# Scores of two attention heads made in turn into two PSUM banks

## The chip, the core and the metric

The kernel runs on one NeuronCore of a Trainium2 chip. TensorE multiplies: it is loaded with a stationary operand (LDWEIGHTS), streams the moving one past it (MATMUL) and writes the product into PSUM, which has 8 banks of 512 f32 values per partition. VectorE (DVE) and ScalarE (ACT) read the banks; GpSimd (POOL) and SyncE (SP) do side work and issue DMAs. The engines run independently and wait for each other on semaphores. The metric is the device time of one execution in microseconds (us), a median over runs.

## What is computed

The reference runs two layers of a first block and two of a second, on 256 tokens of width 1024, in f32. Most of the work is dense projections. The change touches the attention scores of two places:

```python
# dilated attention, group 0 (dilation 1, radius 64): 16 heads of width 64
s = einsum('bqhd,bkhd->bhqk', q, k) * dh ** -0.5 + bias ; p = softmax(s) ; o = p @ v
# second block, differential attention: 8 heads x 2 softmax maps, width 64, causal
q = q.reshape(B, S, DIFF_HEADS, 2, DIFF_HEAD_DIM)      # k likewise; v is (B, S, 8, 128)
o = causal_block_attention(q, k, v, DIFF_HEAD_DIM ** -0.5)
o = o[..., 0, :] - lam * o[..., 1, :]
```

In the kernel each of the 8 x 2 maps is a head of its own, so both places have 16 heads of width 64. The second block runs twice (layers 0 and 1), so there are 16 dilated and 32 differential heads in all.

## The kernel before

`Kernel.order` writes one list of steps, `plan`. `program` walks it, and five generators (`sp_program`, `pe_program`, `act_program`, `dve_program`, `pool_program`) each emit their engine's part of a step, so every engine executes its part of the steps in the list's order. The main thread of the list is a stream of weight tiles: `mm` (12 matmuls of 512 columns, lines 1555 to 1557: weights are split into a high and a low part, `w_hi` and `w_lo`, and the product is made of three terms), followed by `split` for the tile four places on: ACT rounds it to `w_hi` (line 1780) as soon as TensorE is done with the tile whose buffer it takes, and then DVE subtracts to get `w_lo` (line 2060). In the mixers' attention every second `w_lo` is made by POOL (line 2724).

Between tiles a side thread puts attention in. `attention` is a software pipeline, one turn of its loop per weight tile: `scores` of head i, `turn_probs` of head i-1, `values` of head i-2.

- `scores`: TensorE takes a PSUM bank and makes the scores of both blocks of 128 queries (line 1623). Columns 0 to 255 of the bank hold block 1's queries against 256 keys, columns 256 on hold block 0's against 256 keys (dilated) or 128 (causal). DVE adds the bias and takes the maximum (line 2205) and frees the bank; ACT takes the exponential (line 1867).
- `turn_probs`: TensorE waits for the exponential and transposes the probabilities (line 1634), DVE or ACT copies them out (lines 2224, 1887).
- `values`: TensorE multiplies with v (line 1649). The heads of one group share a bank: four in the dilated stage, two in the differential one. Then `keep` or `diff` (line 2670) takes them out.

The operands of a head are 64 partitions high. `qt` and `kt` hold two heads in one chunk of 128 partitions: an even head on partitions 0 to 63, an odd one on 64 to 127 (`at = DH_A * (h % 2)` in the dilated stage, `r = slice(m * DIFF_D, (m + 1) * DIFF_D)` in the differential one). An f32 product that is no transpose shows in the trace as two LDWEIGHTS and two MATMUL records: two passes.

PSUM banks come from one ring, first freed, first taken. `Ring.take` hands TensorE the bank that was freed first, with the event that frees it, and TensorE waits for that event before its next instruction:

```python
bank, given = yield from banks.take(*name)
if given:
    q.wait_ge(*given)
```

One user of the ring is near the change: `oct_scores` (line 1681), the scores of the other two dilated groups. It makes 64x64 products of even and odd heads in turn, into two banks, in four combinations of 64 rows and 64 columns.

Of the kernel before, what the change touches and what calls it, by code (L numbers as in the profile page):

```python
# [17 lines left out]
SEQ = 256  # L18
# [371 lines left out]
class Kernel:  # L390
# [392 lines left out]

    def attention(self, heads, per_bank, by_whom, done):
        n = len(heads)
        for place, h in enumerate(heads):
            h.per_bank, h.place = per_bank, place % per_bank
            h.group = (by_whom, heads[place - h.place].uid)
        for i in range(n + 2):
            if i < n:  # L790
                if heads[i].bias is None:
                    heads[i].raw = self.stat(2)
                self.step("scores", heads[i])
                if heads[i].bias_no is not None and heads[i].bias_no + 6 < H_A:
                    self.step("load_bias", heads[i].bias_no + 6)
            if 0 <= i - 1 < n:
                heads[i - 1].by = self.by_turns()
                self.step("turn_probs", heads[i - 1])
            if i >= 2:
                h = heads[i - 2]  # L800
                self.step("values", h)
                if h.place == per_bank - 1:
                    done(h, i - 2 - h.place)
            yield
# [26 lines left out]
    def dilated(self, i, j):  # L831
# [3 lines left out]
        q, k = self.put("da_q", 0, [P, HALVES, D]), self.put("da_k", 8, [P, HALVES, D])  # L835
# [58 lines left out]
        def dense():  # L894
            yield from need(("v", 0, BLOCK), ("qt", 0, BLOCK), ("kt", 0, BLOCK))
            (qt, kt), v, heads = pairs[0], vs[0], []
            for h in range(H_A):
# [4 lines left out]
                    q=lambda half, c=h // 2, at=at: qt[at:at + DH_A, c, (1 - half) * P:(2 - half) * P],  # L902
# [8 lines left out]

            yield from self.attention(heads, 4, "da", keep)
            got["dense"] = [("vals", heads[-1].uid)]
# [317 lines left out]
    def mix(self, layer, _):  # L1231
# [213 lines left out]
        def attend(kind, per_bank, done):  # L1445
            heads = list(heads_of(kind))
            yield from self.attention(heads, per_bank, kind + L, done)
            got[kind, "vals"] = "vals", heads[-1].uid
# [73 lines left out]
def pe_program(k):  # L1522
# [9 lines left out]
    for what, *of in k.plan:  # L1532
# [6 lines left out]
        if what == "mm":  # L1539
            i, = of  # L1540
# [23 lines left out]
        if what == "mm_chunk":  # L1564
            i, = of
# [50 lines left out]

        if what == "scores":
            h, = of
            bank = yield from bank_for("scores", h.uid)
# [138 lines left out]
def act_program(k):  # L1758
# [8 lines left out]
    for what, *of in k.plan:  # L1767
# [90 lines left out]
        if what == "scores":  # L1858
            h, = of
            bank = yield from banks.of("scores", h.uid)  # L1860
# [178 lines left out]
def dve_program(k):  # L2039
# [11 lines left out]
    for what, *of in k.plan:  # L2051
# [130 lines left out]
        if what == "scores":  # L2182
            h, = of
            bank = yield from banks.of("scores", h.uid)
# [695 lines left out]
```

## Time and profile before

| | us |
|---|---|
| three runs | 2540.09, 2541.14, 2547.57; median 2541.14 |
| the profiled execution | 2539.82, of which the program's span is 2538.5 |
| TensorE busy | 2421.2 (95% of the span) |
| DVE busy | 1480.2 (58%) |
| ACT busy | 1194.4 (47%) |
| DMA | 161 GB/s from HBM over the span |

The 16 dilated heads of group 0 run from 309 to 395 us, the differential heads from 1558 to 1645 us (layer 0) and from 2106 to 2193 us (layer 1). The page gives engine shares over the whole span; what a change inside these three stretches is worth has to be read from the rows of the stretch: the start of one TensorE group to the start of the next gives what a block of work takes, and a bracket such as `[0.68 <-PE banks L1557]` gives how long an engine sat idle before a row, and which work ended that.

### The profile page before, as it was taken

What the parts mean: (1) busy time and instruction counts of PE and PEld (TensorE: products, weight loads), DVE (VectorE), ACT (ScalarE), POOL (GpSimd) and SP (SyncE); (2) the same over time, 40 slices, a digit from 0 to 9 for tenths busy, and PEclk for the clock granted to TensorE, in tenths of its full rate; (3) what the DMA queues carried; (4) which work ended last, traced back from release to release, by engine and by line L of the source; (5) the groups of instructions that cost most, each with busy time, mean ns of one, the idle gap of its engine ahead of it and who ended that gap; (6) DMA issues with size and microseconds to landing.
All of it is one profiled execution on the core that took longest, in us unless ns stands there. A gap on an engine that the chain in (4) does not pass through costs nothing.

```text
span 2538.5 us, 29689 instructions
## 1 busy us (share of the span) xinstructions
PE 2421.2 (95%) x11746; PEld 1957.6 (77%) x11746; DVE 1480.2 (58%) x2158; ACT 1194.4 (47%) x1754; POOL 281.5 (11%) x248
## 2 busy tenths in 40 slices
PE   7998999989999999999999999999999999999999
PEld 5786777768877877777787787777787877887787
DVE  4555556675555547766554577655565576645653
ACT  4443454344434445444444465554554455554543
POOL 1100010000000000000001112333101122333000
PEclk9998999989999999999999999999999999999999
DMA  6765544446556666544566554344556554445554
GB/s 206 204 182 151 175 119 117 144 122 190 175 173 184 181 182 181 160 141 144 176 184 182 181 170 143 108 125 158 179 175 209 179 160 123 117 131 159 169 174 146
DMA packets 211339, 411.36 MB, mean 162 GB/s; under 512 B 13690, under 2 KB 26890, under 8 KB 211200
## 3 DMA queue, kind: packets, MB, share of 16 engines
q1 hardware_dynamic: 204192, 388.55, 51.1%
q0 software_dynamic: 6576, 19.80, 2.9%
q8 instruction: 93, 1.52, 0.2%
q10 hardware_dynamic: 432, 1.11, 0.1%
q14 instruction: 46, 0.38, 0.1%
HBM read 408.31 MB, written 1.10 MB: 161 GB/s over the span
## 4 chain that ended last, share of the span: by engine, by line
PE 81%; DVE 11%; ACT 4%; DMA 2%; issue 2%; POOL 1%; ACTq 0%; DVEq 0%
PE banks L1555 24%; PE banks L1557 23%; PE banks L1556 23%; DVE w_lo L2060 3%; PE banks L1599 2%; ACT w_hi L1780 2%; PE banks L1649 2%; PE banks L1623 1%; PE banks L1634 1%; PE banks L1614 1%; DMA small<-in_diff_lambda 1%; POOL stat L2705 1%; DVE mx_merged L2693 1%; PE banks L1579 1%; PE banks L1580 1%
## 5 line engine op out<-in xcount | busy, mean ns | idle before, releaser
L2060 DVE TENSOR_TENSOR w_lo<-w_raw,w_hi 128x1024 fp32r<-128x1024 f32 x688 | 837.9, 1222 | 862.0 <-ACT w_hi L1780 859.2
L1780 ACT ACTIVATE w_hi<-w_raw 128x1024 fp32r<-128x1024 f32 (+2 forms) x744 | 781.0, 1053 | 974.6 <-PE banks L1557 922.5
L1555 PE MATMUL banks<-w_hi,xt_hi 128*128 128x512 f32 (+3 forms) x2112 | 848.2, 402 | 20.7 <-DVE xt_lo L2088 10.3
L1556 PE MATMUL banks<-w_lo,xt_hi 128*128 128x512 f32 (+3 forms) x2112 | 823.3, 390 | 0.0
L1557 PE MATMUL banks<-w_hi,xt_lo 128*128 128x512 f32 (+3 forms) x2112 | 822.5, 389 | 0.0
L1555 PEld LDWEIGHTS banks<-w_hi,xt_hi 128*128 128x128 f32 x2112 | 403.6, 191 | 111.3 <-issue 18.3
L1557 PEld LDWEIGHTS banks<-w_hi,xt_lo 128*128 128x128 f32 x2112 | 402.3, 190 | 89.1
L1556 PEld LDWEIGHTS banks<-w_lo,xt_hi 128*128 128x128 f32 x2112 | 403.6, 191 | 83.1 <-issue 3.1
L2705 POOL TENSOR_TENSOR stat<-stat,minus_half 128x1 f32<-128x1 f32 (+2 forms) x60 | 54.6, 916 | 1052.4 <-DVE stat L2147 731.3
L2724 POOL TENSOR_TENSOR w_lo<-w_raw,w_hi 128x1024 fp32r<-128x1024 f32 x56 | 134.3, 2399 | 304.4 <-ACT w_hi L1780 304.3
L1555 PE MATMUL banks<-w_hi,ffn_ht_hi 128*128 128x512 f32 x352 | 141.9, 403 | 3.3 <-DVE w_lo L2060 3.3
L1557 PE MATMUL banks<-w_hi,ffn_ht_lo 128*128 128x512 f32 x352 | 140.5, 399 | 0.0
L1556 PE MATMUL banks<-w_lo,ffn_ht_hi 128*128 128x512 f32 x352 | 140.5, 399 | 0.0
L1555 PE MATMUL banks<-w_hi,mlp_ht_hi 128*128 128x512 f32 x256 | 102.2, 399 | 1.2 <-DVE w_lo L2060 1.2
L1557 PE MATMUL banks<-w_hi,mlp_ht_lo 128*128 128x512 f32 x256 | 101.5, 396 | 0.0
L1556 PE MATMUL banks<-w_lo,mlp_ht_hi 128*128 128x512 f32 x256 | 101.4, 396 | 0.0
L1555 PEld LDWEIGHTS banks<-w_hi,ffn_ht_hi 128*128 128x128 f32 x352 | 67.0, 190 | 19.5 <-DVE w_lo L2060 3.7
L1557 PEld LDWEIGHTS banks<-w_hi,ffn_ht_lo 128*128 128x128 f32 x352 | 67.0, 190 | 16.4
L1556 PEld LDWEIGHTS banks<-w_lo,ffn_ht_hi 128*128 128x128 f32 x352 | 67.1, 191 | 15.8
L1599 PE MATMUL banks<-ident,tok 128*128 128x128 f32 x212 | 35.2, 312 | 39.4 <-DVE tok L2068 39.4
L1867 ACT ACTIVATE probs<-probs,mx_nmax 128x256 f32<-128x256 f32 x96 | 42.9, 448 | 63.0 <-DVE mx_nmax L2205 62.8
L1599 PEld LDWEIGHTS banks<-ident,tok 128*128 128x128 f32 x212 | 28.0, 159 | 47.1 <-issue 30.0
(382 smaller groups left out, 2550.0 us busy)
## 6 DMA issues: line engine op xcount, KB each, us to landing
w_raw<-in_w_mlp SPq DMA_DIRECT2D x128, 512.0 KB, 3.8
w_raw<-in_w_in SPq DMA_DIRECT2D x104, 512.0 KB, 3.7
w_raw<-in_ffn_w_gate SPq DMA_DIRECT2D x88, 512.0 KB, 3.7
w_raw<-in_ffn_w_up SPq DMA_DIRECT2D x88, 512.0 KB, 3.8
w_raw<-in_ffn_w_down SPq DMA_DIRECT2D x88, 512.0 KB, 3.7
w_raw<-in_attn_w_in SPq DMA_DIRECT2D x72, 512.0 KB, 3.8
w_raw<-in_ret_w_in SPq DMA_DIRECT2D x64, 512.0 KB, 3.9
w_raw<-in_ret_w_out SPq DMA_DIRECT2D x16, 512.0 KB, 3.9
```

The costliest lines, as they stand in the source:

```text
L1555: pe.matmul(bank, xh, wh, start=(c == 0), stop=False)
L1556: pe.matmul(bank, xh, wl, start=False, stop=False)
L1557: mm = pe.matmul(bank, xl, wh, start=False, stop=(c == b.chunks - 1))
L1579: pe.matmul(bank, xh, hi[:, cols], start=(t.k0 == 0), stop=False)
L1580: pe.matmul(bank, xh, lo[:, cols], start=False, stop=False)
L1599: mm = pe.transpose(bank[:, j * P:(j + 1) * P], src(t.half, s), order)
L1649: mm = pe.matmul(out[:, at:at + h.dv], pt[:, kh, s, :], h.v(kh), start=(kh == 0), stop=(kh == n_keys - 1))
L1780: act.activation(k.w_hi[i % SPLIT][:, 0:m], k.raw[i % RAW][:, 0:m], ACT.Copy).then_inc(*ev.mark(k.w_hi_made, ("w_hi", i)))
L1867: act.activation(row, row, ACT.Exp, bias=h.nmax[:, s:s + 1], scale=-1.0, accum_out=h.den[:, s:s + 1]).then_inc(*done)
L2060: dve.tensor_tensor(lo, raw, hi.bitcast(F32), ALU.subtract).then_inc(*ev.mark(k.w_lo_made, ("w_lo", i)))
L2705: pool.tensor_tensor(out, mean, k.minus_half[:, 0:n], ALU.pow).then_inc(*ev.mark(k.pool_done, name))
L2724: pool.tensor_tensor(lo, raw, hi.bitcast(F32), ALU.subtract).then_inc(*ev.mark(k.w_lo_pool, ("w_lo", i)))
```

## The change

`attention` gets an argument `paired`, true in the two places. For an even head it emits a new step `scores_pair`, in which TensorE makes the scores of the even and of the odd head: it takes a bank for each, and issues block 1 of the even head, block 1 of the odd head, block 0 of the even head, block 0 of the odd head. The step `scores` of both heads stays in its place for DVE and ACT; TensorE passes over it. The products are the same and so are their operands. The other attentions (cross, latent) are not paired.

```diff
-    def attention(self, heads, per_bank, by_whom, done):
+    def attention(self, heads, per_bank, by_whom, done, paired=False):
...
-                self.step("scores", heads[i])
+                if paired and i % 2 == 0:
+                    self.step("scores_pair", heads[i], heads[i + 1])
+                self.step("scores", heads[i], paired)
...
-            yield from self.attention(heads, 4, "da", keep)
+            yield from self.attention(heads, 4, "da", keep, True)
...
-            yield from self.attention(heads, per_bank, kind + L, done)
+            yield from self.attention(heads, per_bank, kind + L, done, kind == "diff")
...
-        if what == "scores":
-            h, = of
+        if what == "scores_pair":
+            both = []
+            for h in of:
+                both.append((yield from bank_for("scores", h.uid)))
+                for e in h.after:
+                    q.wait_ge(*(yield from ev.of(*e)))
+            for s in range(2):
+                for h, bank in zip(of, both):
+                    mm = pe.matmul(bank[:, s * SEQ:s * SEQ + h.keys(s)], h.q(1 - s), h.k[:, 0:h.keys(s)], start=True, stop=True)
+                    if s == 1:
+                        mm.then_inc(*ev.mark(k.pe_done, ("scores", h.uid)))
+
+        if what == "scores" and not of[1]:
+            h, _ = of
```

On TensorE, at the dilated stage's first heads (`da_kt`, `da_qt` are the transposed keys and queries, `probs` the probabilities that are transposed; the weight tile's rows between them repeat), before:

```order
L1623 MATMUL banks<-da_kt_142,da_qt_141 128x256 x2
L1555 MATMUL banks<-w_hi_56,xt_hi 128x512
...
L1623 MATMUL banks<-da_kt_142,da_qt_141 128x256 x2
L1634 MATMUL banks<-ident,probs_72 128x128 x4
L1555 MATMUL banks<-w_hi_53,xt_hi 128x512
...
L1623 MATMUL banks<-da_kt_142,da_qt_141 128x256 x2
L1634 MATMUL banks<-ident,probs_73 128x128 x4
L1649 MATMUL banks<-da_v_145,probs_t_75 128x64 x4
```

and after (line 1627 is the new step, 1648 the transposes, 1663 the values):

```order
L1627 MATMUL banks<-da_kt_142,da_qt_141 128x256 x4
L1557 MATMUL banks<-w_hi_56,xt_hi 128x512
...
L1648 MATMUL banks<-ident,probs_72 128x128 x4
L1557 MATMUL banks<-w_hi_53,xt_hi 128x512
...
L1627 MATMUL banks<-da_kt_142,da_qt_141 128x256 x4
L1648 MATMUL banks<-ident,probs_73 128x128 x4
L1663 MATMUL banks<-da_v_145,probs_t_75 128x64 x4
```

The second head's two products now stand beside the first head's, and the second turn of the loop goes from the weight tile straight to the first head's transposes.

On TensorE in layer 0's differential heads 10 and 11, with what each instruction waits for (`mx_mq` are transposes for the latent attention), before:

```order
L1614 MATMUL banks<-ident,mx_mq_201 96x128 x3
L1623 MATMUL banks<-mx_kt_209,mx_qt_208 128x256 [waits dve_done]
L1623 MATMUL banks<-mx_kt_209,mx_qt_208 128x128
L1634 MATMUL banks<-ident,probs_74 128x128 [waits act_done,dve_done]
L1634 MATMUL banks<-ident,probs_74 128x128 x2
L1649 MATMUL banks<-mx_v_206,probs_t_75 128x128 [waits dve_done]
```

and after:

```order
L1616 MATMUL banks<-ident,mx_mq_201 96x128 x3
L1627 MATMUL banks<-mx_kt_209,mx_qt_208 128x256 [waits dve_done]
L1627 MATMUL banks<-mx_kt_209,mx_qt_208 128x256
L1627 MATMUL banks<-mx_kt_209,mx_qt_208 128x128 x2
L1648 MATMUL banks<-ident,probs_74 128x128 [waits act_done,dve_done]
L1648 MATMUL banks<-ident,probs_74 128x128 x2
L1663 MATMUL banks<-mx_v_206,probs_t_75 128x128 [waits act_done]
```

The pair has taken the ring's bank that the transposes would have had, so everything behind it gets a bank that is freed later: `turn_probs` of head 9 the one that `diff` of heads 6 and 7 frees (line 2670, on DVE), and `values` of head 8 the one that ACT frees when it copies out the first `mx_mq` transposes (line 1821). The rows of DVE, ACT, POOL and SP stand in the same order before and after.

## Rows read from the trace of the kernel before

**Rows 1.** Busy time by stretch: length, PE, PEld, DVE, ACT, POOL, PEclk, DMA, GB/s.

```profile
309.00:395.00 86.00, 85.47 (x452) 66.67 (x451) 46.97 (x100) 42.88 (x98) 10.37 (x20) 1.00 0.45 117
1558.00:1645.00 87.00, 82.06 (x443) 66.68 (x444) 54.89 (x148) 49.23 (x118) 27.61 (x14) 0.98 0.38 107
```

**Rows 2.** Line 1623: count, duration ns min/median/max, first and last start, shapes.

```profile
L1623 PE MATMUL banks<-da_kt,da_qt x64: 376/376/480, 309.8 to 391.0; 64*128 64x256 f32 x64
```

**Rows 3.** PE in order of time, dilated heads: start us, us, what.

```profile
313.53 0.40 PE L1557 MATMUL banks<-w_hi,xt_lo 128*128 128x512 f32 x1
313.85 1.13 PE L1623 MATMUL banks<-da_kt,da_qt 64*128 64x256 f32 x4
314.91 0.66 PE L1634 MATMUL banks<-ident,probs 128*128 128x128 f32 x4
```

**Rows 4.** PE in order of time, layer 0's differential heads.

```profile
1619.79 0.40 PE L1556 MATMUL banks<-w_lo,xt_hi 128*128 128x512 f32 x1
1620.03 0.40 PE L1557 MATMUL banks<-w_hi,xt_lo 128*128 128x512 f32 x1
1620.35 0.92 PE L1623 MATMUL banks<-mx_kt,mx_qt 64*128 64x256 f32 x4
1621.20 0.55 PE L1634 MATMUL banks<-ident,probs 128*128 128x128 f32 x3
```

**Rows 5.** Line 1681 at 404 us: whole group, then its records up to 404.435 and 404.460.

```profile
404.33 1.16 PE L1681 MATMUL banks<-da_kt,da_qt 64*64 64x64 f32 x64
...
L1681 PE MATMUL banks<-da_kt,da_qt x4: 267/267/268, 404.3 to 404.4; 64*64 64x64 f32 x4
...
L1681 PE MATMUL banks<-da_kt,da_qt x8: 218/242/268, 404.3 to 404.5; 64*64 64x64 f32 x8
```

**Rows 6.** Waits from 309 to 395 us: total us, times, longest; then the first of them.

```profile
ACT w_hi L1780 <- PE banks L1557: 7.0, 10, 1.3
...
309.40 1.06 ACT L1780 ACTIVATE w_hi<-w_raw 128x1024 fp32r<-128x1024 f32 x1 [1.17 <-PE banks L1557]
```

**Rows 7.** One turn of the dilated loop in order of time, ACT and PE.

```profile
340.52 1.05 ACT L1780 ACTIVATE w_hi<-w_raw 128x1024 fp32r<-128x1024 f32 x1
...
345.07 0.49 ACT L1867 ACTIVATE probs<-probs,da_nmax 128x256 f32<-128x256 f32 x1
...
346.34 1.06 ACT L1780 ACTIVATE w_hi<-w_raw 128x1024 fp32r<-128x1024 f32 x1 [0.68 <-PE banks L1557]
...
346.95 0.66 PE L1634 MATMUL banks<-ident,probs 128*128 128x128 f32 x4
```

**Rows 8.** Transposes of differential heads 4, 6 and 8 of layer 0 on PE.

```profile
1581.97 0.52 PE L1634 MATMUL banks<-ident,probs 128*128 128x128 f32 x3 [2.17 <-DVE mx_kcat L2625]
...
1592.15 0.55 PE L1634 MATMUL banks<-ident,probs 128*128 128x128 f32 x3
...
1603.50 0.52 PE L1634 MATMUL banks<-ident,probs 128*128 128x128 f32 x3 [1.70 <-ACT probs L1867]
```

**Rows 9.** ACT: the exponential of head 6 ends; the rounding before head 8.

```profile
1591.45 0.19 ACT L1867 ACTIVATION_READ_ACCUMULATOR probs<-probs,mx_nmax 128x1 f32 x1
...
1596.26 1.06 ACT L1780 ACTIVATE w_hi<-w_raw 128x1024 fp32r<-128x1024 f32 x1 [2.22 <-PE banks L1557]
```

**Rows 10.** What frees the banks at heads 10 and 11; PE's values of head 8.

```profile
1610.69 0.69 DVE L2670 TENSOR_TENSOR tmp<-banks,stat 128x512 f32<-128x512 f32 x1
1611.71 0.67 ACT L1821 ACTIVATE mx_mqt<-banks,gain_columns 96x512 f32<-96x512 f32 x1
1611.55 0.83 PE L1649 MATMUL banks<-mx_v,probs_t 128*128 128x128 f32 x6
```

**Rows 11.** Stretches behind PE's long waits, columns as in rows 1.

```profile
1582.00:1590.00 8.00, 7.48 (x41) 6.17 (x42) 4.98 (x16) 5.10 (x12) 2.45 (x2) 1.00 0.24 66
1604.00:1608.00 4.00, 4.00 (x16) 3.39 (x15) 1.63 (x2) 2.86 (x5) 2.10 (x1) 0.57 0.01 4
2130.00:2134.00 4.00, 3.62 (x15) 3.36 (x16) 1.92 (x6) 3.20 (x8) 1.88 (x1) 0.62 0.00 0
```

More of the change, by code:

```diff
@@ L1858, in act_program @@
         if what == "scores":
-            h, = of
+            h, _ = of
             bank = yield from banks.of("scores", h.uid)
@@ L2182, in dve_program @@
         if what == "scores":
-            h, = of
+            h, _ = of
             bank = yield from banks.of("scores", h.uid)
```

## The prediction

> **What bounds the kernel now.** I read the page first: TensorE is busy for 95% of the span, the next engine, DVE, for 58% (the table above). Then the busy times by stretch for the places with paired heads: PE 85.5 us of 86.0 at the dilated heads, 82.1 of 87.0 at layer 0's differential heads, where it idles for 5 us [rows 1]; layer 1's stretch reads alike. So a TensorE microsecond counts there as far as the other engines can follow. Third comes PE's order of time, for what a group of scores takes between its neighbours; fourth the brackets on ACT and PE, for who waits for whom.
>
> **What a group of scores takes.** Tile matmuls start 0.24 us apart (1619.79 and 1620.03 [rows 4]). At the dilated heads the last of a tile starts at 313.53, so PE is free at 313.77, and the transposes start at 314.91: 1.15 us for the scores between them [rows 3]. The group's four passes of 256 columns last 1.13 us and the last alone 0.376, so four starts span 0.757; the first pass is 0.104 longer than the others (480 against 376 ns [rows 2]), which leaves 0.217 us per pass. Four passes are 0.87 us, so 0.28 us go to entering and leaving the group. At a differential head PE is free at 1620.27 and the transposes start at 1621.20: 0.94 us [rows 4]. Two passes of 0.217 and two of half that are 0.65, and again 0.29 is left for entering and leaving.
>
> **What the pair takes.** The edit removes every second group and doubles the passes of the other, with rows 0 to 63 and rows 64 to 127 in turn. No row of before has products 128 columns wide on the two row halves in turn. The nearest is line 1681, which uses both row halves and both column halves: four of its records have started by 404.36, no more until 404.435, and the next four by 404.460; its 64 records last 1.16 us, one of them 0.218 [rows 5]. That is (1.16 - 0.218) / 64 = 15 ns per record, where a pass of 64 columns needs 217 / 4 = 54 ns: four at once, among them two that share their columns and differ in rows. The bounds for the pair: eight passes as long as four (full overlap), or as long as eight (none). I take full overlap, because what two full-width halves share, the columns' way out into two banks, line 1681 shares already. A pair then lasts as long as a single group now, and saves 1.15 us dilated and 0.94 us differential: 8 x 1.15 + 16 x 0.94 = 24.2 us of TensorE, if all of it is kept.
>
> The Trainium skill (TensorE: Matmul & The Clock Gate, Part 3, What overlaps and what doesn't) says that matmuls are strictly first in, first out in their starts and ends. By that, the second pass of one head would hold up the first pass of the next, which is a rival below. The trace speaks against it: each product has two passes, and still four records start together.
>
> **Dilated: what keeps up.** In each turn of the pipeline there is a second loop without TensorE: ACT rounds the next tile (340.52), DVE subtracts and then adds the bias, ACT takes the exponential (its second half at 345.07), and only behind that comes ACT's next rounding (346.34) [rows 7]. TensorE needs 5.4 us per turn (81.2 us between the first and the last of 16 score groups, 309.8 to 391.0 [rows 2]), and would need 4.8. What the loop has to spare is what ACT's roundings wait for TensorE: 7.0 us in the stretch, of which 1.17 lie before the first head [rows 6], so 5.8. The exponential is over at 345.56 and its transposes start at 346.95 [rows 7]: a margin of 1.4 us, from which the odd head's group between them, 1.15, is now taken. So PE will stand before some even heads' transposes, 0.1 to 0.3 us each, and be held to the loop's pace. At the end it may have used up part of the margin; I take 0.4. Of 9.2 us offered, 5.8 + 0.4 = **6.2 us** are kept.
>
> **Differential: what keeps up.** Between the heads DVE and ACT also do the latent attention's norms, and PE stands 2.17 us before the transposes of head 4 and 1.70 before those of head 8 [rows 8]. Layer 0 by pairs, heads 0 to 15:
> - 0 and 1: head 0's exponential is the last thing that its transposes wait for already; 0.
> - 2 and 3: 0.94 gained and lost again before head 4, whose exponential hangs on DVE and ACT waiting for each other; 0.
> - 4 and 5, 8 and 9: PE stands before the first head's transposes; 0.
> - 6 and 7: head 6's exponential is over at 1591.64, its transposes start at 1592.15 [rows 8, 9]; 0.45 gained. It lasts, since the rounding before head 8 waits 2.22 us for PE [rows 9] and moves up with it.
> - 10 to 15: no wait stands before the even heads' transposes, and the norms are done; 3 x 0.94 = 2.8.
> - The new waits: the values of head 8 need the bank that line 1821 frees at 1612.38, and PE reaches them at 1611.55. Before them head 9's transposes need the one that line 2670 frees at 1611.38 [rows 10], which is no later than they start now. Behind the waiting values stands the next tile, and ACT has moved up as far as PE: 0.8 us, of which I count 0.7.
>
> That is 0.45 + 2.8 - 0.7 = 2.6 us. Layer 1 has the same heads in the same order, and I take it alike: **5.2 us** together.
>
> **The clock.** Behind the wait that ended at 1603.50 the next 4 us ran at a granted clock of 0.57, behind layer 1's wait before head 4 at 0.62, and behind the wait that ended at 1581.97 at 1.00 [rows 11]. These waits grow, since the odd head's group no longer stands in them: 2.17 to about 3.7 us with the 0.7 that was gained before. I expect that one to be followed by a dip to 1.2 GHz too: 4 us x 0.43 = 1.7, of which 0.2 lie under the next wait, -1.5 us. In the dilated stretch waits stay too short for that.
>
> **What costs nothing.** DVE, ACT, POOL and SP keep their order. The odd head's scores lie one turn longer in their bank, which the ring of 8 bears everywhere but at heads 8 and 9. DMA moves 107 to 117 GB/s in these stretches [rows 1] and would have to move 8% more; were that cover gone, PE would wait for weight tiles, which it nowhere does there.
>
> **The sum.** 6.2 + 5.2 - 1.5 = 9.9 us off the profiled execution's 2539.8, which is 2529.9. The median of the runs is 1.3 above that execution, so I predict **2531 us**.
>
> **Rivals.**
> - *Half overlap*, 2533. Passes start strictly in order, so a head's second pass runs beside the next head's first: five slots for four, and a pair saves 0.93 dilated and 0.72 differential. Dilated 8 x 0.93 = 7.4 is still above what the loop gives, about 5.7; differential 2 x (0.45 + 3 x 0.72 - 0.7) = 3.8; clock -1.5: 8.0 off. Rows 5 speak against it.
> - *No overlap*, 2538. Full-width products take turns whatever their rows, so the edit doesn't do what it is about; a pair saves one entering and leaving, 0.28: 8 x 0.28 + 2 x (4 x 0.28 - 0.7) = 3.1 off. For it: no row shows two full-width products at once.
> - *Everything kept*, 2517. The other engines follow, 24.2 us off. Against it stand the waits of rows 6 and 8.
> - *Slower*, 2551. Each change of the row half costs what entering and leaving a group costs, 0.28, and nothing overlaps: a pair has three changes and saves one, so it is 2 x 0.28 = 0.56 us longer than two groups are now, 8 x 0.56 + 10 x 0.56 where PE decides, 10 us in all. It decides from a dilated pair longer than 2.3 us. Line 1681 changes halves at every product and shows none of it [rows 5]. The Trainium skill (TensorEngine Tiling (Array Packing), Key Properties) has a drain at a change of tiling mode, "not just tile"; by that too a pair would enter and leave once.
>
> **Chances.** Forecast 0.62, half overlap 0.12, no overlap 0.13, everything or most of it kept 0.09, slower 0.04. Within the forecast the loops may leave 5 to 8 us dilated and 2 to 8 differential, with none to three more dips: 2525 to 2537. A measurement of this kernel can tell a difference of about 0.3%, 7.6 us, from no change. Faster by more: 0.50 + 0.07 + 0.09 = 0.66; within: 0.30; slower by more: 0.04. The range holds the first three cases and some of the fourth: 2522 to 2539.
>
> **What would show it.** The pair's group on PE with its 8 records: 1.1 us long (dilated) and 0.9 (differential) is full overlap, 1.35 and 1.15 half, 2.0 and 1.6 none. In the dilated stretch ACT's roundings hardly wait for PE, PE stands briefly before even heads' transposes, and from the first score group to the last transposes some 6 us are gone, not 9. PE waits 3 us and more before differential head 4, 2.5 before head 8, and the values of head 8 wait. I am wrong in kind if a dilated pair is longer than 1.5 us, and in size if the dilated stretch gives 9 us or a differential one more than 5.

## The result, and the profile after

| | before | after |
|---|---|---|
| median of six runs each, in turn on one chip | 2541.86 (2539.31 to 2547.57) | 2528.67 (2525.50 to 2530.80) |
| the profiled execution / its span | 2539.82 / 2538.5 | 2530.56 / 2529.3 |
| predicted | | 2531 (2522 to 2539) |

The ratio is 0.9945, with a 95% interval of 0.9931 to 0.9958: faster, by more than 0.3%. The two profiled executions are 9.3 us apart, the medians 13.2. In the tables below one of diff_only's eight executions took 2989.8 us at a mean granted clock of 0.75, against about 0.98 in all the others; its median counts it, its ratio does not.

The page of the changed kernel, TensorE's line (busy us, share of the span): 22 us less work than the 2421.2 before, where the pairs offered 24.2.

```profile
PE 2399.1 (95%) x11746; PEld 1946.4 (77%) x11746; DVE 1486.8 (59%) x2158; ACT 1193.3 (47%) x1754; POOL 281.7 (11%) x248
```

So the work is gone nearly as counted, and in the profiled execution more than half of it, 12.9 us, came back as waiting. The two stretches of [rows 1] (columns as there) say where: TensorE now idles for 2.7 us at the dilated heads (0.5 before) and 8.4 at layer 0's differential heads (4.9 before).

```profile
309.00:395.00 86.00, 83.30 (x490) 66.99 (x488) 49.18 (x102) 44.67 (x102) 10.38 (x20) 1.00 0.47 127
1558.00:1645.00 87.00, 78.60 (x448) 65.12 (x447) 59.09 (x143) 47.77 (x112) 30.45 (x16) 0.96 0.37 104
```

The second stretch is that of before, and the changed kernel's differential heads start some 6 us earlier, so their first waits fall out of it. From 1550 to 1645 us TensorE idles for 11.5 us (5.5 before), from 2100 to 2195, around layer 1's heads, for 9.3 (5.5 before). With the dilated heads that is 12 of the 12.9 us.

**The pair.** TensorE in order of time, a dilated and a differential pair, to be held against [rows 3, 4]: eight records where there were four, in the same 1.13 and 0.92 us.

```profile
339.06 1.13 PE L1627 MATMUL banks<-da_kt,da_qt 64*128 64x256 f32 x8
...
1625.72 0.92 PE L1627 MATMUL banks<-mx_kt,mx_qt 64*128 64x256 f32 x8
```

**A dilated turn**, to be held against [rows 7]: ACT and DVE go round without TensorE, from rounding to rounding in 345.29 - 340.25 = 5.04 us, each piece starting as soon as the one ahead of it is done, and TensorE stands for 1.06 us before the even head's transposes, the longest such wait there. ACT's roundings, which waited 7.0 us for TensorE [rows 6], wait 2.1 (the waits of 309 to 391 us).

```profile
340.25 1.05 ACT L1794 ACTIVATE w_hi<-w_raw 128x1024 fp32r<-128x1024 f32 x1
...
341.33 1.23 DVE L2074 TENSOR_TENSOR w_lo<-w_raw,w_hi 128x1024 fp32r<-128x1024 f32 x1 [3.07 <-ACT w_hi L1794]
342.47 0.75 DVE L2132 COPY da_qt<-banks 128x256 f32<-128x256 f32 x2
343.13 0.59 DVE L2219 CUSTOM_DVE_ANT_1 probs<-banks,da_bias 128x256 f32<-128x256 f32 x1
...
344.80 0.49 ACT L1881 ACTIVATE probs<-probs,da_nmax 128x256 f32<-128x256 f32 x1
...
345.29 1.04 ACT L1794 ACTIVATE w_hi<-w_raw 128x1024 fp32r<-128x1024 f32 x1
345.53 0.63 PE L1648 MATMUL banks<-ident,probs 128*128 128x128 f32 x4 [1.06 <-ACT probs L1881]
...
ACT w_hi L1794 <- PE banks L1559: 2.1, 3, 1.2
```

**The differential heads**, layer 0, TensorE's longest waits, to be held against [rows 8, 10]: the transposes of head 0, of head 4 and of head 8, the pair 10 and 11, and the values of head 8.

```profile
1556.58 0.55 PE L1648 MATMUL banks<-ident,probs 128*128 128x128 f32 x3 [1.91 <-ACT probs L1881]
...
1576.66 0.87 PE L1648 MATMUL banks<-ident,probs 128*128 128x128 f32 x3 [3.43 <-DVE mx_kcat L2639]
...
1597.90 0.52 PE L1648 MATMUL banks<-ident,probs 128*128 128x128 f32 x3 [2.55 <-ACT probs L1881]
...
1604.87 0.92 PE L1627 MATMUL banks<-mx_kt,mx_qt 64*128 64x256 f32 x8 [1.65 <-DVE stat L2673]
...
1606.85 1.65 PE L1663 MATMUL banks<-mx_v,probs_t 128*128 128x128 f32 x6 [0.45 <-ACT mx_mqt L1835]
```

The waits of 2.17 and 1.70 us have grown to 3.43 and 2.55, and head 0's transposes wait 1.91; in layer 0 before, the odd head's scores stood in that wait, and they came at 1561.88, right behind the exponential (1561.83). The last row has the new wait for a bank, 0.45 us. The row ahead of it is one that I had not seen: the pair itself takes two banks at once, and by the ring's order the second is the one that DVE frees when it has copied head 8's transposes (1604.17 to 1604.72; the row names DVE's next instruction).

**Where the microseconds are.** The executions of all kernels can be laid beside each other by ACT's roundings of the weight tiles, which every kernel makes in the same order. The table gives, from tile to tile, how much shorter each profiled execution is than the one of before, and behind the slash how much of the clock it lost less (for each stretch of the span in which the granted clock was 0.5, half its length). Tiles 96, 112, 462, 490, 516, 627, 646 and 660 are rounded at 318.9, 404.1, 1541.8, 1673.8, 1773.7, 2106.2, 2202.8 and 2269.4 us before.

| kernel | dilated heads, 96 to 112 | 112 to 462 | layer 0's differential, 462 to 490 | behind them, 490 to 516 | layer 1's, 627 to 646 | behind them, 646 to 660 | whole span |
|---|---|---|---|---|---|---|---|
| changed | 6.4 / 0 | 1.1 / 1.7 | -0.4 / -1.7 | -0.8 / 0 | 2.7 / 0 | 0.0 / 0 | 9.3 / -0.8 |
| after_again | 6.3 / 0 | 3.2 / 5.1 | 2.0 / -1.7 | -0.6 / 0 | 1.2 / 0 | 0.0 / 0 | 12.3 / 4.7 |
| dilated_only | 6.3 / 0 | 2.2 / 1.7 | 0.0 / 0 | 0.0 / 0 | -0.1 / 0 | 0.0 / 0 | 9.5 / 4.2 |
| diff_only | 0.1 / 0 | 0.5 / 0 | 1.2 / -1.7 | -0.8 / 0 | 2.7 / 0 | 0.0 / 0 | 5.0 / -0.6 |
| same_rows | 2.2 / 0 | 3.5 / 5.1 | 0.0 / 0 | -1.4 / -1.7 | 1.5 / 1.7 | 0.0 / 0 | 7.4 / 7.7 |
| head_by_head | 6.3 / 0 | 1.7 / 3.4 | 2.1 / -1.7 | -0.7 / 0 | 2.7 / 0 | 0.0 / 0 | 13.8 / 4.3 |
| pool_paired | 8.1 / 0 | 3.5 / 5.1 | -0.9 / -1.7 | -0.8 / 0 | 2.6 / 0 | 0.0 / 0 | 14.4 / 6.0 |
| pool_before | 0.1 / 0 | 3.1 / 1.7 | -3.9 / -1.7 | -1.2 / -1.7 | -0.3 / 1.7 | 0.0 / 0 | -1.5 / 1.3 |
| lag2 | 6.3 / 0 | 2.9 / 5.1 | -0.8 / -3.4 | -5.0 / -1.7 | 0.4 / -1.7 | -5.4 / -1.7 | -0.4 / -3.4 |
| att_first_before | 0.1 / 0 | 2.2 / 1.7 | 1.1 / 0 | 1.7 / -1.7 | 0.1 / 1.7 | 4.2 / 0 | 13.1 / 5.8 |
| att_first_paired | 6.3 / 0 | 1.9 / 3.4 | 0.8 / -1.7 | 3.0 / 0 | 1.6 / 0 | 4.2 / 0 | 19.7 / 4.0 |
| att_first_pool | 8.1 / 0 | 2.2 / 0 | 2.1 / 0 | 2.3 / 0 | 0.0 / 0 | 4.2 / 0 | 20.1 / 0.6 |
| pool_all | 8.1 / 0 | 3.0 / 5.1 | 4.9 / 0 | 3.8 / 0 | 4.0 / 1.7 | 5.5 / 0 | 32.4 / 9.6 |

The dilated heads repeat to 0.1 us from execution to execution; the differential heads of layer 0 do not, since a fall of the clock lies in them. The stretch 112 to 462 has the same code in all the kernels, and still it is 0.5 to 3.5 us shorter in every other execution than in that of before. Behind layer 0's heads 0.6 to 0.8 us are lost again in all five executions with plain differential pairs, in the last two tiles of the stretch, where TensorE waits for DVE's merged output 3.4 us instead of 3.0; dilated_only has neither. Why DVE is later there isn't shown.

### The profile page after: what moved, and what is told of

Its sections match the earlier page's. It is cut to its first block, busy times and chain, and to the rows that moved or that the text cites. A ratio compares the mean times of both kernels' runs of the same rounds, so it can differ in the third digit from the quotient of the medians.

```text
span 2529.3 us, 29697 instructions
## 1 busy us (share of the span) xinstructions
PE 2399.1 (95%) x11746; PEld 1946.4 (77%) x11746; DVE 1486.8 (59%) x2158; ACT 1193.3 (47%) x1754; POOL 281.7 (11%) x248
## 4 chain that ended last, share of the span: by engine, by line
PE 79%; DVE 12%; ACT 5%; issue 2%; DMA 1%; POOL 1%; ACTq 0%; DVEq 0%
PE banks L1557 24%; PE banks L1558 23%; PE banks L1559 23%; DVE w_lo L2074 3%; ACT w_hi L1794 3%; PE banks L1601 2%; PE banks L1663 1%; PE banks L1648 1%; POOL stat L2719 1%; PE banks L1616 1%; DVE mx_merged L2707 1%; DVE probs L2219 1%; PE banks L1581 1%; ACT probs L1881 1%; DVE tok L2082 1%
```

## Experiments

The kernels of one table were timed in turn with the kernel before on one chip; in the last table pool_all had another, so its ratio is the one to compare.

### Where it comes from, and whether rows are what overlaps

**after_again** is the changed kernel once more.

> The changed kernel once more, to have it beside the others on one chip. The theory: TensorE runs the two row halves side by side, a pair takes as long as one head's scores, and the other engines keep 6 us of it at the dilated heads, 2 to 3 us per differential stretch. The traces of before and after are 9.2 us apart, the medians 13. If the trace is the rule, this kernel is 9 to 10 us faster here too; if the medians are, 13, and 4 us come from somewhere that the two traces do not show.

**dilated_only**:

```diff
-            yield from self.attention(heads, per_bank, kind + L, done, kind == "diff")
+            yield from self.attention(heads, per_bank, kind + L, done)
```

> Pairs in the dilated stage alone. The theory: 6.4 us faster than before (84.6 us from the first scored head to the last transposes became 78.2), so about 2535. If the two places help or hinder each other by the places where the clock falls, the sum of this kernel's gain and diff_only's differs from after_again's by more than 2 us.

**diff_only**:

```diff
-            yield from self.attention(heads, 4, "da", keep, True)
+            yield from self.attention(heads, 4, "da", keep)
```

> Pairs in the differential heads alone. The theory: layer 0 gains 2.6 us less 1.7 for a dip of the clock more (0.9), layer 1 gains 2.8: 3.7 us faster than before, about 2537. If the rest of the measured 13 us comes from the differential heads, this kernel is 6 us faster or more.

**same_rows**:

```diff
-                    mm = pe.matmul(bank[:, s * SEQ:s * SEQ + h.keys(s)], h.q(1 - s), h.k[:, 0:h.keys(s)], start=True, stop=True)
+                    mm = pe.matmul(bank[:, s * SEQ:s * SEQ + h.keys(s)], of[0].q(1 - s), of[0].k[:, 0:h.keys(s)], start=True, stop=True)
```

> The pair as in the changed kernel, two heads in turn into two banks, but the odd head's scores are made from the even head's queries and keys, so all products lie on one row half (the odd heads' scores are thereby not theirs). If row halves are what overlaps, the pair's 8 records start 0.217 us apart, a dilated pair lasts 2.0 us and a differential one 1.6, only 0.28 us per pair is saved, and the kernel is 1 to 3 us faster than before: 2538 to 2540. If it is the two banks that let products overlap, the records start in twos as in the changed kernel and the time is that of after_again.

| | median us | ratio to before (median 2542.75) | 95% interval |
|---|---|---|---|
| after_again | 2527.00 | 0.9936 | 0.9924 to 0.9949 |
| dilated_only | 2532.93 | 0.9960 | 0.9947 to 0.9973 |
| diff_only | 2536.76 | 0.9972 | 0.9962 to 0.9983 |
| same_rows | 2537.69 | 0.9980 | 0.9971 to 0.9989 |

By the ratios the dilated pairs are worth 10 us, the differential ones 7, both 16, each within 3 us: they add as far as that can tell. In the traces the code that differs gains 6.3 us at the dilated heads and 1.2 + 2.7 = 3.9 us at the differential ones, as expected (6.4 and 3.7). The ratios give more, in dilated_only clearly (6.9 to 13.5 us). Its executions lost 4 us less of the clock than those of before, and those of after_again 6, by the mean granted clock of each execution; diff_only's lost no less, and its 3 us more than in the trace stay unexplained.

same_rows settles the overlap. A dilated pair of it on TensorE, a differential one, and line 1627's records for that dilated pair (count, durations, first and last start), with those of the changed kernel behind:

```profile
339.41 1.99 PE L1627 MATMUL banks<-da_kt,da_qt 64*128 64x256 f32 x8
...
1615.79 1.57 PE L1627 MATMUL banks<-mx_kt,mx_qt 64*128 64x256 f32 x8
...
L1627 PE MATMUL banks<-da_kt,da_qt x8: 376/376/480, 339.4 to 341.0; 64*128 64x256 f32 x8
```

```profile
L1627 PE MATMUL banks<-da_kt,da_qt x8: 376/376/480, 339.1 to 339.8; 64*128 64x256 f32 x8
```

The same eight records, two banks in turn, as many columns: with all on one row half, their starts span 1.6 us, on both halves 0.7. A pair lasts 1.99 and 1.57 us against 1.13 and 0.92, as foretold for no overlap (2.0 and 1.6), and the dilated heads gain 2.2 us, which is 8 x 0.28, the price of entering and leaving a group. Two banks alone don't do it; different rows do (whether they would in one bank wasn't run). Only the total is better than the 1 to 3 us expected (5 us, by the ratio's interval 2.8 to 7.4); here too the executions lost 4 us less of the clock than those of before.

### The order in the pair, POOL's share, a longer pipeline

**head_by_head**:

```diff
-            for s in range(2):
-                for h, bank in zip(of, both):
+            for h, bank in zip(of, both):
+                for s in range(2):
```

> The pair into two banks on two row halves, but head by head: both products of the even head, then both of the odd one. If products overlap only where neighbours in the order lie on different row halves (starts are in order), four passes of the even head go 0.216 us apart, the odd head's first runs beside the even head's last, and then three more follow: seven slots, 7 x 0.216 + 0.28 = 1.8 us for a dilated pair, 0.5 us saved, 4 us in all at the dilated heads and 2532 to 2537 in the end. If TensorE keeps work for each row half apart and looks past the order, the pair lasts 1.1 us as in the changed kernel, with 2527.

**pool_paired** (and **pool_before** with the same two lines in the kernel before):

```diff
+            self.share = 2
             yield from self.attention(heads, 4, "da", keep, True)
+            self.share = 0
```

> The changed kernel, and in the dilated stage POOL makes every second w_lo, as it does in the mixers. The theory that DVE and ACT hold the dilated heads back says that TensorE's waits before even heads' transposes go, and that of the 9.2 us offered there all are kept instead of 6.3: the stretch from the first scored head to the last transposes is 75.5 us instead of 78.2, and the kernel 2 to 3 us faster than the changed one, 2524 to 2526. If something else holds it, or POOL at 2.4 us a tile behind its bias loads takes the place of DVE, nothing is gained or some us are lost: 2527 to 2532.

> The same share for POOL, but in the kernel before. There TensorE is busy for 85.5 us of the 86 at the dilated heads, so by the theory nothing can be gained: within 1 us of before. If it is several us faster, what pool_paired gains is not the lifting of a bound that the pairs had run into.

**lag2** (with `lag` 2 for the differential heads and 1 elsewhere):

```diff
-        for i in range(n + 2):
+        for i in range(n + 1 + lag):
...
-            if 0 <= i - 1 < n:
-                heads[i - 1].by = self.by_turns()
-                self.step("turn_probs", heads[i - 1])
-            if i >= 2:
-                h = heads[i - 2]
+            if 0 <= i - lag < n:
+                heads[i - lag].by = self.by_turns()
+                self.step("turn_probs", heads[i - lag])
+            if i >= lag + 1:
+                h = heads[i - lag - 1]
...
-                    done(h, i - 2 - h.place)
+                    done(h, i - lag - 1 - h.place)
```

> The changed kernel, and in the differential heads the transposes of a head come two turns behind its scores instead of one, the values three. The theory says that TensorE stands there for exponentials that come late, not for work that is lacking: in the changed kernel's trace 7.9 us before transposes in layer 0 (4.5 for ACT's exponential, 3.4 for DVE's copy of the keys). With a turn more, most of these waits go and the pairs keep what they save: 4 to 7 us per layer, less about 1 us for a longer tail and for banks that are held longer; 2515 to 2521. If the other engines are as busy as the turns are long, or the banks run out, the waits only move: 2525 to 2530.

| | median us | ratio to before (median 2541.40) | 95% interval |
|---|---|---|---|
| head_by_head | 2527.49 | 0.9951 | 0.9939 to 0.9964 |
| pool_paired | 2525.39 | 0.9937 | 0.9924 to 0.9949 |
| pool_before | 2542.42 | 1.0006 | 0.9996 to 1.0016 |
| lag2 | 2542.05 | 1.0009 | 1.0000 to 1.0018 |

*head_by_head* came out as its second case, the one I had not believed. In the built program the even head's products (256 and 128 columns) stand ahead of the odd head's (256 and 128). Line 1627's first records in a differential pair, up to 1621.8 and up to 1622.0:

```profile
L1627 PE MATMUL banks<-mx_kt,mx_qt x2: 480/480/480, 1621.6 to 1621.6; 64*128 64x256 f32 x2
...
L1627 PE MATMUL banks<-mx_kt,mx_qt x4: 376/428/480, 1621.6 to 1621.9; 64*128 64x256 f32 x4
```

By the program the third and fourth record would be the even head's 128 columns wide; all four are 256 wide, the first two 13 ns apart. So the odd head's first product starts beside the even head's first one, ahead of the even head's second. The pair lasts 0.93 us here and 1.14 at the dilated heads, as in the changed kernel (0.92 and 1.13). Each row half works through its own products, and the starts are not in the order of the program. It follows that the alternation in the change does nothing: the gain comes from the two heads standing together.

*pool_paired* shows the bound at the dilated heads. The stretch 309 to 395 us, and ACT's roundings up to 391:

```profile
309.00:395.00 86.00, 84.98 (x500) 69.29 (x501) 41.48 (x95) 45.08 (x101) 29.41 (x28) 1.00 0.46 127
...
ACT w_hi L1796 <- PE banks L1561: 14.4, 9, 2.3
```

With DVE relieved of every second split, the heads gain 8.1 us instead of 6.3 (expected 9.2), TensorE is busy for 85.0 us of the 86, and it is again ACT that waits for TensorE, 14.4 us instead of 2.1. In pool_before the same relief gives 0.1 us: before the pairs, the loop bound nothing.

*lag2*, at 2542, fell outside both of its cases, and it speaks against my account of the differential heads. The wait for the exponentials was not bought off by a turn more; TensorE's longest waits behind the first heads of layer 0:

```profile
1571.68 0.55 PE L1648 MATMUL banks<-ident,probs 128*128 128x128 f32 x3 [2.07 <-DVE mx_nmax L2219]
1573.07 1.06 PE L1663 MATMUL banks<-mx_v,probs_t 128*128 128x128 f32 x6 [0.84 <-ACT probs_t L1901]
1593.17 0.55 PE L1648 MATMUL banks<-ident,probs 128*128 128x128 f32 x3 [1.43 <-DVE mx_nmax L2219]
1601.79 1.65 PE L1627 MATMUL banks<-mx_kt,mx_qt 64*128 64x256 f32 x8 [3.10 <-ACT probs_t L1901]
1604.57 0.90 PE L1648 MATMUL banks<-ident,probs 128*128 128x128 f32 x3 [1.12 <-DVE mx_mqt L2134]
```

They add up to 8.6 us, against 8.1 in the changed kernel (heads 4 and 8, the pair 10 and 11, the values of head 8), at other heads; over 1550 to 1645 us all waits above 0.1 us are 11.8 against 11.4. The clock falls once more often there, and over its eleven executions lag2 lost some 9 us more of the clock than the changed kernel. The larger loss in the trace, 5.0 and 5.4 us (1.7 of each is clock), lies behind the heads, where all later attention comes a turn later. I had priced that tail at 1 us. That the later turn is what costs there is argued from the place alone.

### DVE's order and DVE's load at the differential heads

Why head 4's exponential is late can be read in the changed kernel, DVE and ACT in order of time: ahead of the scores (L2219) stands a reduction of squares that waits for ACT, which waited 2.70 us for DVE. The exponential is over at 1576.52, 0.04 us before the copy of `mx_kcat` that the row of TensorE's wait names.

```profile
1573.21 0.29 DVE L2594 TENSOR_TENSOR mx_mq<-mx_mq,tmp 128x128 f32<-128x128 f32 x1
1573.54 0.60 ACT L2005 ACTIVATE tmp<-mx_mq 128x480 f32<-128x480 f32 x1 [2.70 <-DVE mx_mq L2594]
1574.17 0.65 DVE L2507 TENSOR_REDUCE norm_sums<-tmp 128x5 f32<-128x480 f32 x1 [0.67 <-ACT tmp L2005]
1574.74 0.47 DVE L2219 CUSTOM_DVE_ANT_0 probs<-banks,causal,head_scale 128x256 f32<-128x256 f32 x1
```

**att_first_paired**, **att_first_before** and **att_first_pool** (the last with POOL's share as in pool_paired):

```diff
-            for g in (prepared, prepared, prepared, attended):
+            for g in (attended, prepared, prepared, prepared):
```

> The changed kernel, and in each turn of the mixers' side work the attention's step is put before the three steps of norms, rotations and transposes instead of behind them. The theory: of the 7.5 us per layer that the pairs offer at the differential heads (8 x 0.94) about 1 to 3 are kept, because DVE takes the scores of heads 4 and 8 only behind a reduction that waits for ACT's squares (0.67 us at 1574.17), so the exponential comes late; the turn more of lag2 moved PE, not DVE's queue. With DVE at the scores first, TensorE's waits before these heads' transposes (7.9 us in layer 0) go, and 4 to 6 us per layer come back: 8 to 10 us faster than the changed kernel, 2516 to 2520. If DVE and ACT have no time left whatever the order, or the norms, now later, hold up the latent attention, the waits only change places: 2524 to 2532.

> The same order of side steps in the kernel before. TensorE idles there for 5 us in the differential stretch of a layer, of which 4 stand before the transposes of heads 4 and 8. By the theory these go: 6 to 9 us faster than before, 2533 to 2536, and the pairs are then worth 16 to 20 us on top of it instead of 14 to 16. If the order of side steps is what the waits hang on in the paired kernel only, this one is within 3 us of before.

> att_first_paired with POOL's share in the dilated stage (pool_paired) as well. The two lie 1100 us apart and should add: 2 to 3 us faster than att_first_paired, 2514 to 2518. If what pool_paired showed was not the dilated stage, it equals att_first_paired.

**pool_all** (on top of att_first_pool, in the mixers' attention):

```diff
-            self.share = 2
+            self.share = 1
```

> att_first_pool, and from the differential heads on POOL makes every w_lo of the mixers instead of every second. What is left of the theory on these heads: not the place of a step, but DVE's load. DVE is busy for 70 us of the 95 around each layer's heads with the attention first, in pieces that wait for ACT and are waited for by PE; TensorE still idles for 8 to 10 us there. Without its share of the splits DVE has some 10 us less to do per stretch. If that load is what keeps the pairs' gain down, TensorE's idle time in 1550 to 1645 and 2100 to 2195 falls by 3 us or more each and the kernel is 5 to 8 us faster than att_first_pool, 2512 to 2515. If it is the length of the norms' chain over ACT, DVE and PE, idle time stays and the kernel is within 3 us; slower if POOL, at 2.4 us a tile and with its own norm steps to make, delivers late.

| | median us | ratio to before | 95% interval |
|---|---|---|---|
| att_first_paired | 2519.86 | 0.9920 (before 2540.80) | 0.9907 to 0.9933 |
| att_first_before | 2530.56 | 0.9959 | 0.9946 to 0.9971 |
| att_first_pool | 2519.68 | 0.9912 | 0.9899 to 0.9925 |
| pool_all | 2509.04 | 0.9874 (before 2543.15) | 0.9853 to 0.9894 |

The total of att_first_paired is about what I expected, its cause is another. At the differential heads it gains 0.8 and 1.6 us, hardly more than the changed kernel in sum, and att_first_before gains 1.1 and 0.1 there, where I had expected some 4 us a layer. The waits changed places (TensorE, layer 0; the first two wait for ACT's copy of `mx_kv` and DVE's rotation, the third for the exponential of another head, the last until DVE's scores):

```profile
1569.33 0.47 PE L1557 MATMUL banks<-w_hi,xt_hi 128*128 128x512 f32 x1 [2.42 <-ACT mx_kv L1807]
1573.27 0.52 PE L1648 MATMUL banks<-ident,probs 128*128 128x128 f32 x3 [0.90 <-DVE mx_mq L2590]
1585.09 0.55 PE L1648 MATMUL banks<-ident,probs 128*128 128x128 f32 x3 [3.00 <-ACT probs L1881]
...
1604.52 0.64 PE L1616 MATMUL banks<-ident,mx_mq 128*96 128x128 f32 x4 [2.29 <-DVE mx_nmax L2219]
```

The gain lies behind them, in the cross and latent attention: 3.0 and 4.2 us, and att_first_before gains 1.7 and 4.2 there without any pair. By the medians the pairs are worth 10.7 us on top of the new order (6.6 in the traces), not 16 to 20. The pairs' 13 to 16 us on the old order hold 3 to 6 us of clock, and on the new one the mean granted clock is the same with and without them, so most of the shortfall can be that. Whether the order and the pairs also draw on the same idle time isn't shown. att_first_pool did not show its 2 to 3 us in the median (0.2; 2.0 by the ratios), though its dilated heads gained the 8.1 us again; four executions of each, with intervals of 3 us to either side, can't tell. Its trace lost 3.4 us more of the clock than att_first_paired's.

pool_all is the fastest kernel of the study, 34 us below before, about 10 below att_first_pool by the ratios, where 5 to 8 were expected; by the mean granted clock of the executions some 4 of the 10 can be clock. In the traces 2.8, 1.5, 4.0 (1.7 of it clock) and 1.2 us lie in the four stretches at and behind the differential heads. The stretch of layer 0 in att_first_pool, then in pool_all:

```profile
1550.00:1645.00 95.00, 85.66 (x494) 70.39 (x495) 70.68 (x157) 53.35 (x127) 30.77 (x16) 0.98 0.42 118
```

```profile
1550.00:1645.00 95.00, 88.27 (x509) 72.95 (x510) 68.51 (x145) 56.43 (x133) 57.81 (x28) 0.98 0.39 111
```

TensorE idles 6.7 us instead of 9.3 (layer 1: 6.4 instead of 8.7), a little under the 3 us that I had set as the mark. So DVE's share of the splits is one of the things that keep the pairs' gain down, and not the only one. DVE's busy time went down by 2 us only, although it made ten splits of 1.22 us less; the last section has most of the reason.

## Why the prediction was right

- **The bound and the group's price.** Right: four passes at 0.217 us and 0.28 for entering and leaving. same_rows measures both by themselves (2.2 us for eight entries and leavings saved).
- **Full overlap, from line 1681.** Right, and 1.13 and 0.92 us are what was forecast. The rivals "half overlap", "no overlap" and "slower" fall with the trace and with same_rows; head_by_head shows that the reason given for half overlap, starts in the program's order, doesn't hold even where the program gives a reason to wait. The Trainium skill (TensorE: Matmul & The Clock Gate, Part 3, What overlaps and what doesn't) has matmuls start and end strictly in order; the first two records of head_by_head, 13 ns apart, speak against it for products of two passes on two row halves.
- **Dilated, 6.2 us.** Measured 6.3 to 6.4 in every kernel with these pairs and DVE's splits as before. The mechanism, a loop of ACT and DVE of 5 us, is shown by pool_paired and pool_before. That the sum 5.8 + 0.4 fits so closely is partly luck: ACT's roundings gave up 7.0 - 2.1 = 4.9 us of their waits, not 5.8, so 1.5 us came from elsewhere, where 0.4 was taken. TensorE's waits before even heads are three, of 0.45, 1.06 and 0.51 us, not many of 0.1 to 0.3.
- **Differential, 5.2 less 1.5 for the clock.** The sum is close: 3.7 forecast, 3.9 in diff_only, 2.2 in the changed kernel, 3.2 in after_again, 4.8 in head_by_head, 1.7 in pool_paired (both layers, the clock included), 3.2 in the mean. The waits came as said: before head 4 3.43 us (said 3.7), before head 8 2.55 (2.5), at head 8's values 0.45 (0.7 to 0.8). Heads 0 and 1 were taken to gain nothing, and what left the space before head 0's transposes is a wait there, 1.91 us. One fall of the clock more in layer 0, 1.7 us, behind the wait before head 4, is in all five traces with plain pairs there (1.5 was taken); of the three traces with the old scores there, before and dilated_only do not have it, but pool_before has. One step was missed: a pair takes two banks at once, and at heads 10 and 11 the second is freed by DVE's copy of head 8. That is 1.65 us in layer 0 of the changed kernel and of pool_paired and 1.66 in layer 1 of after_again, where the clock did not fall behind head 8; it is 0.4 us at most where it fell there (0.32 in layer 1 of the changed kernel, 0.14 in layer 0 of after_again), since TensorE came later anyway. The stretches with the wait gained -0.4, -0.9 and 1.2 us, those without it 1.2 to 2.7. Also missed were the 0.6 to 0.8 us lost again behind layer 0's heads. "DVE keeps its order, so it costs nothing" left out that the instructions meet others on POOL than before (last section); what that costs wasn't separated.
- **Everything kept, 2517.** Wrong for this kernel: of 22 us less work 9.3 stayed in the traces. At the dilated heads POOL's share shows that it is the others that have to follow.
- **The sum and the median.** 9.9 us off the profiled execution, 9.3 measured, of which 6.4 and 2.2 are at the pairs; the rest is the net of 1.1 us between tiles 112 and 462, 0.8 lost behind layer 0's heads and smaller ones, which the forecast had at nothing. The forecast of 2531 is 2.3 us above the median because of its last term: "the median of the runs is 1.3 above that execution", taken alike for both kernels. With more runs, the profiled execution of before lies 1.0 to 3.3 us under its medians (2540.80 to 2543.15; 2541.86 in the comparison above), and the changed kernel's profiled one 1.9 above its own: 9.3 + 2.0 + 1.9 = 13.2. I had taken one execution against three runs as firm to a microsecond, and the clock outside the three stretches as the same in both kernels, which it is not (below).

**The clock over many executions.** Each execution has its mean granted clock on record. The 58 executions of before in the experiments' tables have 0.9820 in the mean, and their times go with it: 2547.0 us in the mean of the four at 0.980, 2541.2 of the 26 at 0.982, 2538.1 of the two at 0.984. The twelve of the changed kernel (six here, six as after_again) have 0.9833, which over 2540 us is 3.4 us less lost, about what the medians show beyond the traces. At equal clock, 0.984, it takes 2527.2 us (nine executions), 10.9 less than before. In the changed kernel, after_again, dilated_only, head_by_head and pool_paired, all with dilated pairs, 20 of 28 executions have 0.984; of before's 58 five have that or more, of the 18 of pool_before and diff_only none. So the median's further 4 us came with the dilated pairs, as less time at the lower clock. They were in no term of the forecast; that the range held them too is luck. It is no rule of the pairs: with the attention first they change nothing (0.9828 with them, 0.9827 without), and in lag2, which has them, the clock is lower than before (0.9798). The clock of an execution is on record to 0.001 only, which is 2.5 us; the means are surer than one execution.

**What stays open.** Why less time is lost to the clock with dilated pairs: no run takes that apart. And at the differential heads neither a turn more, nor another order, nor less work for DVE took away more than 3 us of TensorE's idle time each; the rest of their bound wasn't found.

## What to carry to other kernels

Two heads' f32 products with operands 64 partitions high, on different row halves and into different banks, cost TensorE what one head's cost, if they stand next to each other; of the two orders among them that were run neither was better. Before pairing, ask in each stretch what loop runs without TensorE and how long a turn of it is: that pace, and not the work saved, set the gain at the dilated heads (6.3 of 9.2 us), and moving a piece of DVE's work to an idle engine was worth 1.8 us after the pairs and nothing before them. Before a forecast to a tenth of a per cent, look at how one kernel's executions scatter: here the profiled one was 1 to 3 us under its median.

## What the runs showed of the hardware

**Starts out of the program's order.** In head_by_head the third product of the program started 13 ns behind the first, ahead of the second, since its row half was free (rows above).

**The clock falls elsewhere from execution to execution.** Between tiles 112 and 462, with the same code, before lost 25.6 us to a granted clock of 0.5 (1.2 GHz) and the others 20.5 to 25.6. A fall is not always paid: in the changed kernel's layer 0 it did not fall behind head 8, TensorE came early and stood 1.65 us for a bank; in after_again it fell there and 0.14 us of the wait was left. In layer 1 it is the other way round: 0.32 us with the fall in the changed kernel, 1.66 without it in after_again.

```profile
2148.54 0.92 PE L1627 MATMUL banks<-mx_kt,mx_qt 64*128 64x256 f32 x8 [1.66 <-DVE stat L2673]
```

**DVE stands still beside POOL.** POOL's split and DVE's scaling of two columns, in the changed kernel, and the groups of that scaling over 1550 to 1645 us (busy, mean ns), in the changed kernel:

```profile
1588.00 2.40 POOL L2738 TENSOR_TENSOR w_lo<-w_raw,w_hi 128x1024 fp32r<-128x1024 f32 x1
1588.02 2.41 DVE L2676 TENSOR_SCALAR stat<-stat,lam 128x2 f32<-128x2 f32 x1
...
L2676 DVE TENSOR_SCALAR stat<-stat,lam 128x2 f32<-128x2 f32 x8 | 7.9, 989 | 0.3
```

and in the kernel before and in att_first_pool:

```profile
L2662 DVE TENSOR_SCALAR stat<-stat,lam 128x2 f32<-128x2 f32 x7 | 4.4, 622 | 0.2
```

```profile
L2678 DVE TENSOR_SCALAR stat<-stat,lam 128x2 f32<-128x2 f32 x8 | 12.2, 1519 | 0.3
```

The instruction takes 0.23 us by itself. Where it meets POOL's split it ends when the split ends, 2.41 us at the longest; DVE's instructions that read a bank were not lengthened (L2219: 411 ns in the mean), nor were the reduction of squares (L2507) and the reciprocal (L2673), which do not read one: at most 14 ns beside a split. Counted over all DVE instructions of layer 0's differential stretch, 1550 to 1645 us, that is 3.9 us before, 8.8 in the changed kernel, 15.6 in att_first_paired, 14.8 in att_first_pool and 23.1 in pool_all (21.6 in layer 1). So 8 of the 12 us that ten splits less would save DVE came back as stalls. The Trainium skill (Perfetto Trace Analysis, Optimizing Scalar/DVE Operations) warns that moving work from DVE to GpSimd might not help because the two share a read port of SBUF. The trace has stalls of DVE beside POOL, 2.41 us for 0.23 at the longest, and the move was still worth 10 us by the ratios (some 4 of them perhaps clock).
